# Mixed order of gate, up and down weights in the expert stream of a MoE trunk

## The reference

```python
hg = jnp.einsum('nd,edf->nef', t, wg)
hu = jnp.einsum('nd,edf->nef', t, wu)
act = jax.nn.silu(hg) * hu * combine[:, :, None].astype(t.dtype)
out = jnp.einsum('nef,efd->nd', act, wd)
```

## Time and profile before

| | |
|---|---|
| runs (three) | 2173.23 us median, 2168.86 to 2173.33 |
| the profiled execution | 2173.65 us, of which 2172.0 us are the profile's span |
| PE, DVE, ACT, POOL busy | 89%, 76%, 66%, 4% of the span |
| granted PE clock over the span | 0.949 |
| a window inside the expert stream (900 to 932 us) | DVE 30.04 of 32 us busy, PE 29.95, ACT 27.14; clock 1.00; DMA share 1.01, 400 GB/s |
| DVE low parts | 384 read from `proj` slots in the two expert streams, 640 from `raw` slots, 1219 ns each |

### The profile page before, as it was taken

One profiled execution on the slowest core, in us unless ns is written; L12 is line 12 of the kernel. 1 busy time (PEld: TensorE's weight loads), 2 busy tenths in 40 slices (PEclk: granted clock), 3 DMA queues, 4 the chain that ended last, 5 costly groups with the idle time before them and its releaser, 6 DMA issues.

```text
span 2172.0 us, 31270 instructions
## 1 busy us (share of the span) xinstructions
PE 1926.3 (89%) x8974; PEld 1489.1 (69%) x8974; DVE 1649.0 (76%) x2365; ACT 1429.4 (66%) x2272; POOL 89.9 (4%) x86
## 2 busy tenths in 40 slices
PE   7999998976999999999499999989689999999993
PEld 6877776765766667667377777768566667666662
DVE  5467666556999999999465667665569999999994
ACT  5555565344888888888355565653358888888882
POOL 0000000001000000000000000000000000000000
PEclk9999999986999999999789999999779999999996
DMA  6434443545999999999544444435469999999993
GB/s 255 153 136 166 147 153 117 180 188 204 380 377 381 402 388 389 391 396 383 198 145 146 141 157 164 141 117 194 176 231 374 397 381 394 384 379 391 385 375 135
DMA packets 83003, 575.13 MB, mean 265 GB/s; under 512 B 11760, under 2 KB 12016, under 8 KB 13264
## 3 DMA queue, kind: packets, MB, share of 16 engines
q1 hardware_dynamic: 75600, 542.01, 65.4%
q0 software_dynamic: 7296, 31.85, 4.4%
HBM read 567.52 MB, written 23.07 MB: 272 GB/s over the span
## 4 chain that ended last, share of the span: by engine, by line
PE 55%; issue 15%; DVE 13%; ACT 12%; DMA 3%; ACTq 1%; DVEq 1%; POOLq 0%; POOL 0%; SPq 0%
PE bank L767 9%; PE bank L769 9%; PE bank L768 9%; DVE wl L1084 7%; PE bank L932 6%; PE bank L934 6%; PE bank L933 6%; ACT wh L520 6%; ACT rows L717 4%; PE bank L916 2%; PE bank L918 1%; PE bank L907 1%; PE bank L899 1%; DMA proj<-picks 1%; ACT xh L691 1%
## 5 line engine op out<-in xcount | busy, mean ns | idle before, releaser
L1084 DVE TENSOR_TENSOR wl<-raw,wh 128x1024 fp32r<-128x1024 f32 x640 | 765.2, 1219 | 328.0 <-ACT wh L520 326.8
L520 ACT ACTIVATE wh<-raw 128x1024 fp32r<-128x1024 f32 x640 | 663.8, 1056 | 423.8 <-PE bank L769 342.1
L916 PE MATMUL bank<-wh,xh 128*128 128x512 f32 x1024 | 444.1, 434 | 68.3 <-DVE wl L1084 64.2
L1084 DVE TENSOR_TENSOR wl<-proj,wh 128x1024 fp32r<-128x1024 f32 x384 | 452.9, 1217 | 48.8 <-ACT wh L520 48.1
L520 ACT ACTIVATE wh<-proj 128x1024 fp32r<-128x1024 f32 x384 | 393.7, 1055 | 79.1 <-PE bank L934 62.7
L767 PE MATMUL bank<-wh,xh 128*128 128x512 f32 x1024 | 419.5, 410 | 6.0 <-DVE xl L1121 3.1
L918 PE MATMUL bank<-wl,xh 128*128 128x512 f32 x1024 | 410.7, 401 | 0.0
L769 PE MATMUL bank<-wh,xl 128*128 128x512 f32 x1024 | 405.2, 396 | 0.0
L768 PE MATMUL bank<-wl,xh 128*128 128x512 f32 x1024 | 404.3, 395 | 0.0
L916 PEld LDWEIGHTS bank<-wh,xh 128*128 128x128 f32 x1024 | 196.4, 192 | 207.2 <-DVE wl L1084 167.7
L767 PEld LDWEIGHTS bank<-wh,xh 128*128 128x128 f32 x1024 | 196.0, 191 | 49.5 <-DVE wl L1084 9.9
(11 more groups left out here) (208 smaller groups left out, 1596.6 us busy)
## 6 DMA issues: line engine op xcount, KB each, us to landing
raw<-in_expert_units SPq DMA_DIRECT2D x192, 1024.0 KB, 7.9
proj<-in_expert_units SPq DMA_DIRECT2D x192, 1024.0 KB, 8.0
raw<-in_in_units SPq DMA_DIRECT2D x96, 1024.0 KB, 4.8
raw<-in_out_units SPq DMA_DIRECT2D x32, 1024.0 KB, 4.8
proj<-picks POOLq DMA_DIRECT2D x8, 1024.0 KB, 8.0
expert_rows<-rows POOLq DMA_DIRECT2D x4, 1024.0 KB, 4.3
x<-in_x SPq DMA_DIRECT2D x2, 1024.0 KB, 6.5
wide<-in_norms POOLq DMA_DIRECT2D x2, 1024.0 KB, 5.0
```

Source lines behind the costliest of these rows:

```text
L520: act_(wh[:, h % CUT, :], ring[j][:, h % 2 * HALF:(h % 2 + 1) * HALF], ACT.Copy)\
L916: mm(bank[m][:, :], stacked[b][:, 2 * h + c, :], wh[:, h % CUT, k], start=(h + c == 0), stop=False)
L1084: v.tensor_tensor(wl[:, h % CUT, :], ring[(first + h // 2) % slots][:, h % 2 * HALF:(h % 2 + 1) * HALF], wh[:, h % CUT, :].bitcast(F32), A ...
```

## The change

The 12 units of a step stand in another order: gate, gate, up, gate, down, gate, down, up, down, up, down, up, as pieces `gggguuggddggdduudduudduu`. The host lays the units out in this order, and PE picks the piece's kind from the same string. The gate is now complete after piece 11 instead of 7, and the gate's tasks move with it: ACT's copy behind cut 15, PE's turn behind piece 13, the exponential behind cut 17, DVE's three jobs behind cuts 18, 19 and 20. Down is complete after piece 21, and its four stores move into the next step, behind cuts 1, 2, 4 and 6. Up still ends with piece 23; its tasks and those of the gathered rows keep their places. The first step keeps its order, and the 8 down pieces of the last expert still follow at the end; the stores of the down results before them are moved out beside those.

```diff
-GATE_OUT = PART + CUT - 1
-GATE_TURN = PART + 1
+PLAN = {True: "g" * PART + "u" * PART, False: "gggguuggddggdduudduudduu", None: "d" * PART}
+GATED_AT = {first: PLAN[first].rindex("g") for first in (False, True)}
+GATE_OUT = {first: at + CUT for first, at in GATED_AT.items()}
+GATE_TURN = {first: at + 2 for first, at in GATED_AT.items()}
 UP_OUT = CUT - 1
 UP_TURN = 1
-STORE = {2 * PART + CUT - 1: 0, 2 * PART + CUT: 1, 2 * PART + CUT + 1: 2, 2 * PART + CUT + 2: 3}
+STORE = {PLAN[False].rindex("d") + CUT - 3 * PART + k: n for n, k in enumerate((0, 1, 3, 5))}
...
-                        if h in STORE and not first:
-                            store(1 - b, STORE[h], k - 1)
+                        if h in STORE and stores:
+                            store(b, STORE[h], k - 2)
...
                 with t_.one_round():
-                    step(0, 0, first=True)
-                    with t_.loop(e.Fori(0, NE // 2 - 1)) as i:
-                        step(1, i * 2 + 1)
+                    step(0, 0, first=True, stores=False)
+                    step(1, 1, stores=False)
+                    with t_.loop(e.Fori(0, NE // 2 - 2)) as i:
                         step(0, i * 2 + 2)
+                        step(1, i * 2 + 3)
+                    step(0, NE - 2)
                     step(1, NE - 1, last=True)
                     for h in range(PART):
                         cut(h, DEEP, 4)
+                        if h == 1 or h == 2:
+                            store(0, h - 1, NE - 2)
                         if h == UP_OUT:
                             up_out()
+                            for k in (2, 3):
+                                store(0, k, NE - 2)
                             act_hi()
...
             def step(b, first=False, last=False):
-                for h in range((2 if first else 3) * PART):
-                    if h < PART:
-                        up_half(b, 0, h)
-                    elif h < 2 * PART and not first:
-                        down_half(h - PART)
+                for h, part in enumerate(PLAN[first]):
+                    n = PLAN[first][:h].count(part)
+                    if part == "d":
+                        down_half(n, h % CUT)
                     else:
-                        up_half(b, 1, h % PART)
+                        up_half(b, "gu".index(part), n, h % CUT)
...
-                        if h == GATE_OUT + 3:
+                        if h == GATE_OUT[first] + 3:
                             gate_plus()
-                        if h == GATE_OUT + 4:
+                        if h == GATE_OUT[first] + 4:
                             gate_inverse()
-                        if h == GATE_OUT + 4 if first else h == GATE_OUT + 5:
+                        if h == GATE_OUT[first] + (4 if first else 5):
                             gate_silu()
...
-    order = [gate[:, 0], up[:, 0]]
+    experts = [gate[:, 0], up[:, 0]]
     for k in range(1, NE):
-        order += [gate[:, k], down[:, k - 1], up[:, k]]
-    experts = np.concatenate(order + [down[:, NE - 1]], 1)
+        taken = {"g": iter(range(F // P)), "u": iter(range(F // P)), "d": iter(range(F // P))}
+        for part in PLAN[False][::2]:
+            n = next(taken[part])
+            experts.append({"g": gate[:, k], "u": up[:, k], "d": down[:, k - 1]}[part][:, n:n + 1])
+    experts = np.concatenate(experts + [down[:, NE - 1]], 1)
```

More of the change, by code:

```diff
@@ L720, in store, with step @@
                         ins.then_inc(S["out_ready"], 1)
-                def step(b, k, first=False, last=False):
+                def step(b, k, first=False, last=False, stores=True):
                     at = 0 if first or b == 1 else 4
-                    for h in range((2 if first else 3) * PART):
+                    for h in range(len(PLAN[first])):
                         cut(h, DEEP, at)
@@ L732, in step @@
                             act_hi()
-                        if h == GATE_OUT:
+                        if h == GATE_OUT[first]:
                             gate_out()
-                        if h == GATE_OUT + 2:
+                        if h == GATE_OUT[first] + 2:
                             gate_exp()
@@ L909, in turn_act, with up_half @@
                 last.then_inc(S[turned], 1)
-            def up_half(b, m, h):
+            def up_half(b, m, h, j):
                 e.wait_ge(S["lo_ready"], t_.due("lo_ready"))
@@ L915, in up_half, with down_half @@
                     k = slice(c * COLS, (c + 1) * COLS)
-                    mm(bank[m][:, :], stacked[b][:, 2 * h + c, :], wh[:, h % CUT, k], start=(h + c == 0),
+                    mm(bank[m][:, :], stacked[b][:, 2 * h + c, :], wh[:, j, k], start=(h + c == 0),
                        stop=False)
-                    last = mm(bank[m][:, :], stacked[b][:, 2 * h + c, :], wl[:, h % CUT, k], start=False,
+                    last = mm(bank[m][:, :], stacked[b][:, 2 * h + c, :], wl[:, j, k], start=False,
                               stop=(h == PART - 1 and c == 1))
                 last.then_inc(S["cut_free"], 1)
-            def down_half(h):
+            def down_half(h, j):
                 if h == 0:
@@ L931, in down_half @@
                     o = bank[2 + 2 * (h % 2) + c][:, :]
-                    mm(o, actT[:, k, 0:STACK], wh[:, h % CUT, r], start=(k == 0), stop=False)
-                    mm(o, actT[:, k, 0:STACK], wl[:, h % CUT, r], start=False, stop=False)
-                    last = mm(o, actT[:, k, SLOTS:SLOTS + STACK], wh[:, h % CUT, r], start=False, stop=(k == 3))
+                    mm(o, actT[:, k, 0:STACK], wh[:, j, r], start=(k == 0), stop=False)
+                    mm(o, actT[:, k, 0:STACK], wl[:, j, r], start=False, stop=False)
+                    last = mm(o, actT[:, k, SLOTS:SLOTS + STACK], wh[:, j, r], start=False, stop=(k == 3))
                 last.then_inc(S["cut_free"], 1)
@@ L959, in step @@
                         turn_act(4 * SLOTS, "up_out", "up_turned")
-                    if h == GATE_TURN:
+                    if h == GATE_TURN[first]:
                         turn_act(0, "gate_out", "gate_turned")
@@ L1071, in _ @@
                     for h in range(PART):
-                        down_half(h)
+                        down_half(h, h % CUT)
         @block.vector
```

## The result

| | before | changed |
|---|---|---|
| runs | 2172.94 us median of 4 (2168.86 to 2173.33) | 2145.88 us median of 4 (2141.55 to 2150.52) |
| profiled execution, span | 2173.65, 2172.0 | 2144.65, 2143.0 |
| ratio to before | | 0.9882, 95% interval 0.9868 to 0.9897 |
| period of an expert step | 33.73 us | 32.81 us |

The forecast was 2149.6 us; measured 27.1 us less than before instead of 23.6. In two later groups of runs, each beside runs of the kernel before, the same kernel had the ratios 0.9907 (0.9890 to 0.9923) and 0.9898 (0.9881 to 0.9916), 20.7 and 20.5 us less. I take about 1% as the size. All runs compared by time here are of the fast state.

The account below looks back on a forecast made before the run. No engine alone bounds the kernel; a loop of PE, DVE and ACT does. Steps of 32.84 instead of 33.73 us save 25.7, loads return 2: 2173.65 - 25.7 + 2 = 2150, less 0.4 is 2149.6 us; range 2138 to 2161.

Parts of the forecast that it names:

- the gap before piece 14: DVE's wait for ACT, which waits for PE in the block of eight down pieces; 0.94 us lost before the change.
- before 17: New DVE gap before piece 17, after down piece 13 and the gathered turn on PE; 0.63 us lost.
- before 18: DVE gap before piece 18, since the act turn now follows piece 13 on PE; 0.10 us.
- at piece 6: DVE gap while ACT waits for the gated product and copies act before its cut; 0.70 us lost, as before.
- between 18 and the next 4: DVE's pieces 18 to the next step's 4, where 0.76 us about pieces 20 to 23 was lost; no gap left.
- ACT's wait for the down matmuls before cut 17: ACT's cuts waiting on down matmuls, 1.17 us at 929.09 before; about half of that expected after the change.
- the margin of 0.07 from cut 1 to cut 4: ACT's cut 4 reaches DVE at 26.81, DVE is free at 26.88; stores hidden, any further microsecond passes through in full.
- 14 intervals and the end: Per layer, 14 intervals each 0.89 us shorter and an end 0.37 earlier; 25.7 us over two layers.
- the term: Time the loads give back once steps are shorter; between 0 and 5 us in all, 2 taken.
- the third rival: Scatter, now far from the gather, starves the loads by a second dip; 2232 us, chance 0.15 with lesser forms.
- the time to landing: How long a load takes to land; to rise from 8.0 to some 9 or 10 us.
- a lead of 10: Loads' lead over use, 22.5 us slot reuse less 8.0 to land and about 4 in use; some 10 us.

Follow-up runs that it names:

- Run 1: Kernel before with its old piece order, only the four down stores moved behind cuts 1, 2, 4 and 6 of the next step; 2152.46 us, ratio 0.9908.
- run 5: Changed kernel with one more ACT copy, result thrown away, behind the store that follows cut 2; 2156.03 us, ratio 0.9937.
- 6: Changed kernel with three of the four stores of each step left out inside the stream; 2711.4 us, containing a second round; period 32.80.
- run 3: Changed kernel with a gather that takes only token 0; first layer's stream 516.85 against 520.21 us (time 2713.38 us means nothing).
- the early turn: Changed kernel with the first half of the gathered rows' turn moved from behind piece 12 to behind piece 5; 2142.53 us, ratio 0.9858; later 0.9867.
- run 8: Changed kernel with the gather replaced by a plain copy of the first 64 rows; only first layer read, two intervals 33.64 and 34.16 us.

## Why the prediction was right

**The period.** Forecast 32.84, measured 32.81. Piece by piece: the gap before piece 14 is gone; before 17 it was to be 0.63 and is 0.74, before 18 0.10 and is 881.69 - 881.01 - 0.60 = 0.08; at piece 6 0.70 and is 0.64; between 18 and the next 4 none, and there is none. One sign did not come: ACT's wait for the down matmuls before cut 17, 1.17 before, was to be about half of that and is 1.08 in steps without a wait for a landing. Runs 1, 5 and 6 moved the parts apart: the stores alone give 33.00 (33.05 to 33.1 expected), one copy more costs 0.47 (0.50), three stores fewer give 0.01. Of the margin of 0.07 from cut 1 to cut 4 run 5 finds nothing, and the rows of the changed kernel show 0.04.

**The sum.** 14 intervals and the end were to shorten a layer's stream by 12.8 us before the loads take theirs. Without rows in the gather the first layer's stream is 516.85, 14.2 under 531.00. 1.6 of that lie in the interval that I had counted as unchanged, the first, which went from 34.15 to 32.58; part of it is only that the fourth gather of run 3 came late, 5.16 us behind the third instead of 4.02. From the fifth gather on run 3 takes 484.27 us after 496.85, 12.6 less, where the sum says 12.8. With rows the changed kernel's three first layers take 487.15, 487.35 and 484.25, so the loads take 2.9, 3.1 and nothing, 2.0 us on the mean. I took 1, in a range of 0 to 2.5: the term was small by a factor of two, and it varies from run to run by more than its mean.

**What failed: the reading of the slow stretch.** In the part on the loads, and as the argument against the third rival, I put 243 GB/s down to the scatter, because its window, 872 to 875, stood behind a scatter at 871.98. The gather had gone out 4.26 us before. Where the two now stand 15 us apart, the slow stretch follows the gather and nothing follows the scatter; run 3, where it goes with the gather's rows, shows it. The changed kernel, 858 to 861 (5 us behind a gather) and 867 to 870 (the scatter goes out at 867.68):

```profile
DMA packets 100, 0.68 MB, mean 227 GB/s; under 512 B 17, under 2 KB 17, under 8 KB 17
```

```profile
DMA packets 172, 1.25 MB, mean 418 GB/s; under 512 B 19, under 2 KB 19, under 8 KB 19
```

The forecast escaped this because it used only the loss per step, not its owner. The third rival did not come, since there was only ever one dip to separate. Nor did the time to landing rise to "9 or 10", but to 17 and more. That sign did not even follow from my own sum, which had 14 steps use up 12.5 us of a lead of 10. Run 1 shows the other side: at 33.00 the loads keep up in both layers, at 32.81 they just don't.

**What the order is worth.** The addition gave it 0.2 a step, the loop keeps it (33.00 to 32.81), and the loads take it back: 2.7 us a layer by the period, 0.7 in the streams (520.0 to 519.3), nothing from the fifth gather on (486.2 in both), not measurable in the time. The gain that can be measured is that of the stores. The loads are no fixed end, though: the early turn shortens the loop by 0.33 a step more, 4.6 us a layer, and 3.3 to 3.7 of them arrive in the streams. That the waits for landings cost the one gain nearly whole and the other only in part is not explained here.

**The time.** The medians of the three groups, 2145.88, 2149.6 and 2148.46, lie at or under the forecast of 2149.6, but the kernel before had lower medians in the later groups too; the gains are 27.1, 20.7 and 20.5 us for the 23.6 forecast. That agreement is partly luck: the clock that stays up in the first step of the first layer, which I did not foresee, gives some 4 us, the loads take more than I gave them, and of the profiles' 29.0 us only the streams' 22.0 are what the prediction worked out, as 25.7 less 2.

## What to carry to other kernels

When three engines pass buffers in a ring, write down for each piece when each engine can take it, from start to start; the idle time of the busiest engine in one period then comes out to a tenth of a microsecond, and so does what an edit moves. Side jobs of an engine belong where another engine is busy with something long; crowding them between the last use of a buffer and the next chain is free only up to the slack of the ring. Before a faster loop is counted over all steps, compare the loads' need per step with the new period, and carry the difference to the last step: here the loads took back the 0.19 us a step of the mixed order, and about a quarter of the next 0.33.

## What the runs showed of the hardware

- A copy or gather of up to 64 rows of 8 KB on GpSimd's queue into 64 partitions, beside a stream of 1 MB loads, lowers the whole rate from about 421 GB/s to 220 to 350 for some 4 to 9 us. In the changed kernel the windows 855 to 864 carried 352, 227 and 303 GB/s, so about 3 x (69 + 194 + 118) GB/s us = 1.1 MB, or 2.7 us, were lost for a gather of at most 0.5 MB. This was the worst of seven steps; they lost 0.6 to 1.1 MB, 0.8 on the mean, or 1.9 us. The plain form and another source do the same.
- With nothing beside them, copies of 64 rows of 8 KB on GpSimd's queue moved 240 GB/s (run 8, 495 to 498 us), copies of 128 such rows on the same queue 429 (1066 to 1072 us).
- A scatter of as many rows to DRAM costs nothing that these windows show (418 GB/s).
- In the first expert step of the first layer PE's clock, once up, stayed up in two programs and fell back to its lower level for 9 us or more in others with the same order there (0.50 against 1.00 between 515 and 520 us), with PE shown as busy throughout.
- The DMA share reads about 1.0 in the expert stream of the kernel before (0.97 to 1.01 in windows of a step, 381 to 397 GB/s), 1.00 to 1.02 in the changed one and 0.97 to 1.00 in run 3, whether a load takes 8 or 17 us to land; it does not tell how much room is left. The time to landing through the layer does.
